# Attention heads of a decoder layer: product banks emptied in mid-step into two buffers, scores issued one and a half tiles ahead

## The reference, cut to what matters

```python
proj = h @ w_in                      # q, k, v of both groups, 16 heads of 64
# group A, 8 "stick-breaking" heads (called SB here)
z = q @ k.T * d ** -0.5              # strictly causal
weights = exp(log_sigmoid(z) + later)    # later: sum of log_sigmoid(-z) over later keys before q
o = weights @ v
# group B, 8 rotary heads with dilated windows (called DIL here)
q, k = rotary(q), rotary(k)
o = softmax mixture over three (window, dilation) patterns of q @ k.T, times v
```

## Time and profile before

| what | value |
|---|---|
| median of 3 runs | 2114.16 us (2113.18 to 2114.74) |
| the profiled execution's own time | 2112.07 us |
| its span, first to last instruction | 2110.3 us |
| PE busy over the span | 1929.9 us (91%) |
| DVE, ACT, POOL busy | 1250.9, 903.0, 731.9 us |
| mean granted clock of TensorE | 0.961 |
| stretch of the heads' steps | about 724 to 1330 us |

### The profile page before, as it was taken

The page is one execution under the profiler, slowest core; times in us unless marked ns, Lnnn a source line. Parts: engine busy times, 40 slices in busy tenths (PEclk is TensorE's granted clock), DMA queues, the critical chain, the costliest instruction groups (busy, mean ns, idle before and its releaser), DMA issues. The chain is left out here.

```text
span 2110.3 us, 25935 instructions
## 1 busy us (share of the span) xinstructions
PE 1929.9 (91%) x9224; PEld 1580.6 (75%) x9224; DVE 1250.9 (59%) x1665; ACT 903.0 (43%) x1451; POOL 731.9 (35%) x490
## 2 busy tenths in 40 slices
PE   5899999999998978978888876797899999999998
PEld 4788888888887767767667665586688888888886
DVE  6855555555556266657666578336955556555555
ACT  6433333333335345545545556305433333333334
POOL 2656556540000241231231235402656656540000
PEclk9999999999999989989989997898999999999999
DMA  3443534458664210111111012512443534458663
GB/s 141 161 163 134 195 130 172 158 204 294 194 195 159 70 42 26 36 40 29 30 40 40 25 36 70 185 40 80 144 165 132 195 147 156 174 190 309 194 195 140
DMA packets 95574, 275.93 MB, mean 131 GB/s; under 512 B 10480, under 2 KB 14704, under 8 KB 89840
## 3 DMA queue, kind: packets, MB, share of 16 engines
q1 hardware_dynamic: 95472, 274.59, 38.2%
HBM read 190.14 MB, written 80.22 MB: 128 GB/s over the span
## 5 line engine op out<-in xcount | busy, mean ns | idle before, releaser
L703 PE MATMUL banks<-ffn_x_operands_hi 128*128 128x512 f32 x616 | 239.8, 389 | 0.0
L706 PE MATMUL banks<-ffn_x_operands_hi,ffn_x_operands_lo 128*128 128x512 f32 x616 | 239.7, 389 | 0.0
L705 PE MATMUL banks<-ffn_x_operands_lo,ffn_x_operands_hi 128*128 128x512 f32 x616 | 239.6, 389 | 0.0
L1376 PE MATMUL banks<-first_hi,w_hi 128*128 128x512 f32 x384 | 163.6, 426 | 58.9 <-ACT heads_rot_in L1113 42.8
L1244 DVE TENSOR_TENSOR heads_wt<-banks,heads_wt 128x512 fp32r<-128x512 f32 (+1 forms) x160 | 101.0, 633 | 171.3 <-ACT heads_wt L1091 171.1
L991 POOL TENSOR_TENSOR w_lo<-w_raw,w_hi 128x1024 fp32r<-128x1024 f32 x22 | 52.5, 2385 | 362.3 <-ACT w_hi L1055 362.3
L984 POOL TENSOR_TENSOR scaled_rows<-scaled_rows,heads_stay 128x128 f32<-128x128 f32 (+7 forms) x64 | 86.0, 1350 | 237.5 <-DVE heads_stay L1204 237.5
L401 ACT ACTIVATE scaled_rows<-banks 128x512 f32<-128x512 f32 x132 | 78.9, 598 | 203.4 <-PE banks L690 203.4
L516 DVE TENSOR_TENSOR scaled_rows<-banks,scaled_rows 128x512 f32<-128x512 f32 x132 | 91.2, 691 | 117.7 <-PE banks L690 73.5
L1091 ACT ACTIVATE heads_wt<-banks 128x512 fp32r<-128x512 f32 (+1 forms) x160 | 88.8, 555 | 166.2 <-PE banks L1427 165.4
L1378 PE MATMUL banks<-first_hi,w_lo 128*128 128x512 f32 x384 | 157.9, 411 | 0.0
(11 more groups left out here) (183 smaller groups left out, 4854.6 us busy)
## 6 DMA issues: line engine op xcount, KB each, us to landing
w_raw<-in_ffn_w_gate SPq DMA_DIRECT2D x22, 1024.0 KB, 6.8
ffn_up_raw<-in_ffn_w_up SPq DMA_DIRECT2D x22, 1024.0 KB, 6.2
ffn_down_raw<-in_ffn_w_down SPq DMA_DIRECT2D x22, 1024.0 KB, 4.9
down_operands<-ffn_down_raw SPq DMA_DIRECT2D x22, 1024.0 KB, 7.3
w_raw<-h_operands SPq DMA_DIRECT2D x52, 256.0 KB, 2.9
ffn_up_raw<-h_operands SPq DMA_DIRECT2D x52, 256.0 KB, 3.0
ffn_down_raw<-h_operands SPq DMA_DIRECT2D x50, 256.0 KB, 3.0
w_raw<-in_w_in SPq DMA_DIRECT2D x24, 512.0 KB, 3.9
```

The source lines that it names most:

```text
L703: pe.matmul(out, hi[:, 0, tok], hi[:, 1, :], start=(opens and c == 0), stop=False, skip_group_check=True)
L705: pe.matmul(out, hi[:, 0, tok], lo[:, 1, :], start=False, stop=False, skip_group_check=True)
L706: last = pe.matmul(out, lo[:, 0, tok], hi[:, 1, :], start=False, stop=(c == NP - 1), skip_group_check=True)
L1376: pe.matmul(out, hi[:, k, :], norm.xn_hi[:, k, cols], start=(k == 0), stop=False)
```

## The change

Three things change together. First, `UNITS` is rewritten so that products 0 to 4 end before a step's bank (bank 0 in step 1, bank 1 in steps 2 to 5) and no longer behind its last one; `ENDS` keeps the same steps. Second, every q and k product is copied by ACT at once into `qk_raw[j % 2]` and the PSUM bank is free with that copy, for both kinds; the SB kind's high part is then made by ACT from this buffer, and its low part by POOL instead of DVE. `rot_swap` becomes two buffers as well. Third, PE issues `scores(s+2)` within step s, ahead of its last bank (behind the only bank in steps 0 and 1) and before that bank's projection units, where before `scores(s+1)` opened the step.

```diff
-UNITS = ((2, 2), (2, 2), (2, 4, 2), (3, 2, 3), (2, 1, 3, 2), (2, 1, 3, 2), (2, 1, 3, 1, 0), (0, 0, 1, 0, 0))
+UNITS = ((3, 2), (3, 2), (3, 3, 2), (3, 3, 2), (3, 3, 2, 0), (3, 3, 2, 0), (2, 2, 1, 0, 0), (0, 0, 1, 0, 0))
...
-        rot_in, rot_swap, rot_out = sb("rot_in", [P, HALF]), sb("rot_swap", [P, HALF]), sb("rot_out", [P, HALF])
+        qk_raw = [sb(f"qk_raw{i}", [P, HALF]) for i in range(2)]
+        rot_swap, rot_out = [sb(f"rot_swap{i}", [P, HALF]) for i in range(2)], sb("rot_out", [P, HALF])
...
+            def projected_lo(it, j):
+
+                piece, half = PRODUCTS[j]
+                cols = slice(half * HALF, (half + 1) * HALF)
+                pool.wait_ge(sb_hi_done, ROTATED * it + j + 1)
+                pool.tensor_tensor(qk_lo[SB_KIND][piece][:, cols], qk_raw[j % 2][:, :],
+                                   qk_hi[SB_KIND][piece][:, cols].bitcast(F32), ALU.subtract).then_inc(sb_split, 1)
...
-                if project and kind1 == DIL_KIND and ENDS.get(s, HALVES) < ROTATED:
-                    rotate_cos(it1, ENDS[s])
+                if project and ENDS.get(s, HALVES) < ROTATED:
+                    if kind1 == DIL_KIND:
+                        rotate_cos(it1, ENDS[s])
+                    else:
+                        projected_lo(it1, ENDS[s])
...
-                elif kind == SB_KIND:
-                    act.activation(qk_hi[kind][piece][:, cols], b.ps[:, bank, :], ACT.Copy
-                                   ).then_inc(sb_hi_done, 1)
                 else:
-                    act.wait_ge(rot_split, 1 + ROTATED * it + j)
-                    act.activation(rot_in[:, :], b.ps[:, bank, :], ACT.Copy).then_inc(proj_free, 1)
+                    if kind == DIL_KIND:
+                        act.wait_ge(rot_split, 1 + ROTATED * it + j - (j > 0))
+                    if kind == SB_KIND and (j > 1 or not (isinstance(it, int) and it == 0)):
+                        act.wait_ge(sb_split, ROTATED * it + j - (j > 0))
+                    act.activation(qk_raw[j % 2][:, :], b.ps[:, bank, :], ACT.Copy).then_inc(proj_free, 1)
+                if piece != V and kind == SB_KIND:
+                    act.wait_ge(proj_free, 1 + HALVES * run(it, kind) + j + 1)
+                    act.activation(qk_hi[kind][piece][:, cols], qk_raw[j % 2][:, :], ACT.Copy).then_inc(sb_hi_done, 1)
...
-            def projected_lo(it, j, bank=BANK_PROJ):
...
+            def scores_ahead(it, kind, s, last):
+
+                if s + 2 < STEPS:
+                    scores(it, kind, s + 2)
+                elif not last:
+                    scores(*pair_of(it, kind, 1), s + 2 - STEPS)
+
             def step(it, kind, s, proj=True, last=False):
                 it1, kind1 = pair_of(it, kind, 1)
-                nit, nkind, ns = (it, kind, s + 1) if s < STEPS - 1 else (it1, kind1, 0)
-                if not (last and s == STEPS - 1):
-                    scores(nit, nkind, ns)
+                early = max(banks_of(s) - 1, 1)
...
                 for j in range(banks_of(s)):
+                    if j == early:
+                        scores_ahead(it, kind, s, last)
                     if proj:
                         project(it1, kind1, *units_between(s, j))
                     turn_weights(it, kind, s, j, proj)
                     values_behind(it, kind, s, j, 2)
+                if early == banks_of(s):
+                    scores_ahead(it, kind, s, last)
                 if proj:
                     project(it1, kind1, *units_between(s, banks_of(s)))
...
             scores(0, SB_KIND, 0)
+            scores(0, SB_KIND, 1)
```

More of the change, by code:

```diff
@@ L850, in heads_block @@
         proj_ready, proj_free = sem("proj_ready"), sem("proj_free")
-        sb_hi_done = sem("sb_qk_hi_done")
-        rot_swapped, rot_cos, rot_sin, rot_sum = (sem(f"rot_{n}") for n in ("swapped", "cos", "sin", "sum"))
+        sb_hi_done, sb_split = sem("sb_qk_hi_done"), sem("sb_qk_split")
+        rot_swapped = [sem(f"rot_swapped{i}") for i in range(2)]
+        rot_cos, rot_sin, rot_sum = (sem(f"rot_{n}") for n in ("cos", "sin", "sum"))
         rot_hi_done, rot_split = sem("rot_hi_done"), sem("rot_split")
@@ L915, in swap_halves @@
                         dst = head * HEAD + (1 - part) * 32
-                        sp.dma_start(rot_swap[dst:dst + 32, :], rot_in[src:src + 32, :]
-                                     ).then_inc(rot_swapped, 16)
+                        sp.dma_start(rot_swap[j % 2][dst:dst + 32, :], qk_raw[j % 2][src:src + 32, :]
+                                     ).then_inc(rot_swapped[j % 2], 16)
             def store_part(it, kind, part):
@@ L999, in rotate_cos @@
                 pool.wait_ge(rot_split, 1 + n)
-                pool.tensor_tensor(rot_out[:, :], rot_in[:, :], cos_sb[:, half * HALF:(half + 1) * HALF],
+                pool.tensor_tensor(rot_out[:, :], qk_raw[j % 2][:, :], cos_sb[:, half * HALF:(half + 1) * HALF],
                                    ALU.mult).then_inc(rot_cos, 1)
+            def projected_lo(it, j):
[4 more added lines that the diff above has]
+                                   qk_hi[SB_KIND][piece][:, cols].bitcast(F32), ALU.subtract).then_inc(sb_split, 1)
             def step(it, kind, s, project=True, last=False):
@@ L1033, in one_run @@
                         split_out_weights(s)
-            split_weights(0, 0, V)
-            split_weights(0, 1, Q)
+            for j in range(HALVES):
+                if j < ROTATED:
+                    projected_lo(0, j)
+                if j == 2:
+                    split_weights(0, 0, V)
+                if j == 3:
+                    split_weights(0, 1, Q)
             pool.wait_ge(tables_ready, 1)
@@ L1267, in values_out @@
                                   ).then_inc(o_copied, 1)
-            def projected_lo(it, j, bank=BANK_PROJ):
[L1271 to L1274, removed]
-                                  qk_hi[SB_KIND][piece][:, cols].bitcast(F32), ALU.subtract
-                                  ).then_inc(proj_free, 1)
             def rotate(it, j):
@@ L1281, in rotate @@
                 n = ROTATED * it + j
[L1282 to L1283 removed]
+                dve.wait_ge(rot_swapped[j % 2], 64 * (ROTATED // 2 * it + j // 2 + 1))
+                dve.tensor_tensor(rot_swap[j % 2][:, :], rot_swap[j % 2][:, :], sin_sb[:, cols], ALU.mult).then_inc(rot_sin, 1)
                 dve.wait_ge(rot_sin, n + 1)
                 dve.wait_ge(rot_cos, n + 1)
[L1286 removed]
+                dve.tensor_tensor(rot_out[:, :], rot_out[:, :], rot_swap[j % 2][:, :], ALU.add).then_inc(rot_sum, 1)
             def rotated_lo(it, j):
@@ L1309, in step @@
                 for j in range(banks_of(s)):
-                    if project and kind1 == SB_KIND and ends_before(s, j) and ENDS[s] < ROTATED:
-                        projected_lo(it1, ENDS[s])
                     weights_lo(it, kind, s, j, project)
@@ L1325, in step @@
                     rotated_lo(*rot)
-                if project and kind1 == SB_KIND and ends_before(s, banks_of(s)) and ENDS[s] < ROTATED:
-                    projected_lo(it1, ENDS[s])
                 if last and s == STEPS - 1:
@@ L1386, in scores @@
                     if kind == SB_KIND:
-                        pe.wait_ge(proj_free, 1 + HALVES * run(it, kind) + (2 if s == 0 else 4))
+                        pe.wait_ge(sb_split, ROTATED * it + (2 if s == 0 else 4))
                     else:
```

5 lines of the change are left out of this document (removed).

## The result

| what | before | after |
|---|---|---|
| median | 2114.45 us (2113.18 to 2114.74, 4 runs) | 2179.72 us (2178.85 to 2180.09, 4 runs) |
| ratio | | 1.0309, 95% interval 1.0291 to 1.0327 |
| profiled execution, its span | 2112.07, 2110.3 us | 2179.71, 2177.9 us |
| TensorE's mean granted clock | 0.961 | 0.951 |

What follows compares the result with a forecast made beforehand. PE was taken to bound DIL runs, a ring of in-order engines SB runs. 2112.07 + 18.6 (DIL) + 8 (SB) = 2138.7 us profiled, 2141 us as median; the 8-in-10 range was 2090 to 2165 us.

Steps and rivals of the forecast that it cites:

- The added wait: DIL steps 0 to 3: PE stands at early scores until the next tile's second head is read, 7.9 us per run.
- What was taken away: PE's waits for `rot_in`, v and low-part copies end: 12.8 us per SB run; with a score wait, 3.4 per DIL run.
- DIL runs: New waits 7.9 us against 3.4 gone, plus 1.7 for the clock: +6.2 us per run, +18.6 for three.
- SB runs: Three parts of the run, 2.7 - 1.8 - 0.6, plus 1.7 for the clock: +2.0 us per run, +8 for four.
- the last run: Without units, transposes about 2 us later in steps 2, 3, about 1.5 earlier in 4 to 6: 0, bounds -5 and +5.
- the transitions: No own term; from the fourth rotation to an SB run's end, the v copy no longer precedes the gates: -0.6 us.
- Rival D: DVE and POOL collide over POOL's new low parts, 6.4 us in each of three DIL runs: 2160 us, chance 0.05.
- The clock: One 3.4 us spell at 1.2 GHz per DIL run, behind the 3.0 us wait, costs 1.7 us; SB runs also +1.7.
- The ring: In-order engines waiting on each other bound SB runs from tile 2's transposes to the fourth rotation: 51.7 against 53.5 us.
- B: `rotated_hi` is ready when ACT comes, gates are not late; SB runs lose 15.7 us each: about 2070 us, chance 0.22.
- C: No change: no clock spells (-15 us) and a ring 3 us shorter per run: 2114 us, chance 0.09.
- The signs to look for: Expected profile: raw-copy waits under 1 us, score waits on gates and maximum, DIL clock spells, run lengths, ACT idle 4 us.

Runs made afterwards that it cites:

- fourth experiment: The changed kernel with the SB kind's low parts made by DVE again instead of POOL: 2177.58 us, ratio 1.0298.
- the first experiment: The changed kernel with scores(s+1) opening step s again; new `UNITS`, early copies, two buffers and POOL's low part stay: 2082.19 us, ratio 0.9848.

## Why the prediction was right in sign and wrong in size

**The added wait, right.** "It waits until both heads of tile s+1 are read. But the second head is read only behind the copy of bank (s, 0), which PE has just transposed." That holds, in place and in size: forecast 0.8, 3.0, 2.5, 1.6 us in a DIL run, measured 0.83, 3.02, 2.69, 1.68. Reading the heads in another order takes the DIL loss away, and confining the early scores to steps 4 to 6 nearly all of it in SB and DIL runs and half of it in the last.

**What was taken away, right in after.** No unit waits for a copy any more. Alone, this part brings 32 us, but not as forecast: it leaves 11.0 us of waits for copies, takes 7 to 10 us from an SB run and makes a DIL run 1.0 us longer, not 3.4 shorter. In after those 11.0 us are gone too; that PE stands at the scores while the copies are made is my reading and was not tested.

**Which terms failed.** The sum for the profiled execution is 41.0 us too low (2138.7 for 2179.71). DIL runs have 18.5 of that (18.6 forecast, 37.1 measured), SB runs 10.0 (8 and 18.0), the last run 8.6 (0 and 8.6), the transitions 3.6, for which there was no term. The steps that failed are the two short waits called covered, the spells counted as one, DVE's outputs left out in SB runs, and the gain expected in the last run.

**DIL runs, term too small: +6.2 forecast, +12.3 measured.** Waits and clock explain it. PE's idle time in the run rose from 3.4 us before to 11.7 (71.02 - 59.36). Of this, 8.2 us were the four foreseen waits, and 2.1 were in steps 4 and 5, of which I wrote "have three units and a whole bank between and are covered". They are covered while a normalisation takes 0.6 us, not 2.7. Another 1.4 us of idle time stayed, where I had counted all 3.4 as gone. *Rival D named the mechanism, at 6.4 us per run, and looked at the wrong operation.* I asked what POOL would newly do, and that makes no difference (fourth experiment). What collides is what POOL did already, moved in time by `UNITS`. The remaining 4.1 us are busy time (59.36 - 55.26), of which the clock has 3.4.

**The clock, one spell for two.** The forecast put one spell of 3.4 us behind the wait of 3.0 us. There is one behind each of the two longest waits, 3.02 and 2.69 us. Busy time by stretch, after, the 3.4 us behind the starts at 1000.56 and 1010.07:

```profile
1000.80:1004.20 3.40, 3.40 (x11) 2.26 (x10) 1.85 (x6) 0.64 (x2) 0.00 (x0) 0.50 0.85 199
1010.80:1014.20 3.40, 3.40 (x15) 2.62 (x12) 0.00 (x0) 0.00 (x0) 0.00 (x0) 0.53 0.00 0
```

In both PE is busy all through, at 1.2 of 2.4 GHz, and loses half of it: 3.4 us per run against the 1.7 taken. The two spells lay inside the bounds that I gave ("two or three spells, 5 us"), and the forecast took one.

**SB runs, term too small: +2.0 forecast, +4.2 in the run shown, 18.0 for four against 8.** The ring was the right picture, and the waits at the scores came out *shorter* than forecast, 12.5 us for 15.3. Missing were two other waits. Waits of PE, after, the SB run from 896.76 to 979.38 us:

```profile
PE banks L1411 <- ACT heads_stay L1083: 12.5, 6, 3.9
PE banks L1454 <- DVE heads_o_stage L1287: 2.9, 1, 2.9
PE banks L1433 <- DVE heads_wt L1265: 1.9, 2, 1.3
```

The same stretch before has 10.7 us for `rot_in`, 2.0 for v and 0.7 for POOL, 13.4 in all, against 17.3 here: +3.9 us. The 4.8 us behind DVE are not the scores' doing: with the scores in their old place they are there too (4.0 and 0.8 us). With the old `UNITS` and the same buffers there are 1.1 us of them, so they come with the new `UNITS`. I had counted only the chain through ACT and gave DVE's outputs no new wait. The clock's term of +1.7 did not come: PE's busy time is 64.3 us before and 64.5 after in this run, at 0.89 and 0.90.

**Transitions.** I counted each run up to its last step, and "from there to the run's end" at -0.6. The stretch from step 7's mark to the next run's step 0 grew instead by 0.9 us four times. Busy time by stretch, after:

```profile
979.38:988.02 8.64, 7.58 (x43) 6.85 (x44) 4.50 (x13) 5.58 (x12) 1.44 (x1) 0.75 0.00 0
```

Before it is 7.75 us with PE busy for 5.72 at clock 1.00. What is new is a spell at 1.2 GHz from 976.87 to 983.70, behind the wait of 2.90 us for DVE's output that ended at 975.93. Two experiments place it: with the scores in their old place the stretch still takes 8.59 us at clock 0.68, and with the old `UNITS` as well 7.76 us at 1.00. It comes with the new `UNITS`.

**The last run, term with its bounds too small: 0 with -5 to +5 forecast, +8.6 measured.** The forecast set two scores of about 2 us later against three banks of about 1.5 us earlier. Waits of PE, after, the last run:

```profile
PE banks L1433 <- DVE scaled_rows L1251: 11.6, 9, 2.5
PE banks L1411 <- DVE heads_row_max L1236: 8.7, 6, 2.5
PE banks L1454 <- DVE heads_o_stage L1287: 2.7, 2, 1.6
```

Before it is 4.7, 3.7 and 8.6 us. PE is late at the transposes as well as at the scores; I take it that without units nothing uses the lateness up, which no experiment isolates. The gain in steps 4 to 6 is there only in the 8.6 that fell to 2.7, and on the whole it is a loss: early scores from step 4 on alone make this run 5.1 us longer (61.15 for 56.04). The clock fell from 0.74 to 0.70.

**Rivals.** B, "the ring opens", got 0.22. For after it is wrong, and yet it describes the first experiment: SB runs of 69 us at clock 0.92 to 0.97. "SB runs near 70 us with the clock near 1.0" is what the buffers and the new `UNITS` do when the scores stay. I priced the two parts together, in the ring: -1.8 us from the start of tile 2's transposes to the fourth rotation. In fact the one part takes 9 us off an SB run (78.38 to 69.07) and the other puts 13.5 on. C has no support, and its clock spells come to 12 us by the sum's own terms (seven of 1.7), not 15.

**The signs to look for.** Right: no wait on the raw copy; 51.8 us at the scores for gates (40 to 60 forecast); clock spells in DIL runs; ACT idle before each `rotated_hi`, though for 2.0 to 4.8 us and not always 4. Wrong: 39.5 us for the maximum (20 to 30 forecast), DIL runs of 79.4 us from step 0's mark to the next run's (71 to 75), and SB runs of 89.9 to 91.3 us in the same way (84 to 90).

**What stays open.** How the 13.5 us that the scores' place costs an SB run divide between waits and clock is known only in parts. Taking `rotated_hi` out of the way removes 24 us of gate waits over all runs, but 22 return through POOL, and that return was not taken away by itself. Why `UNITS` moves the weight split in DIL runs was not followed link by link either; the runs show only that it does.

## What to carry to other kernels

Issuing work earlier into a double buffer can move a wait instead of removing it: look up where in its own queue the engine that frees the buffer reads it, and compare that with the work that still lies behind the issue on the first engine. Split a change into its parts before it is judged, since here -32 and +97 us were in one diff. When a change shifts the timing of a step, ask not only what each engine newly does beside the others, but which old operations now fall beside one another.

## What the runs showed of the hardware

- DVE and POOL held each other up by whole instructions, in both directions. A normalisation on SBUF of 0.55 us takes 2.73 us when POOL's split of 2.39 us starts just ahead of it; POOL's split of 2.38 us takes 5.05 when a scan and a rotation of DVE fall inside it, although by the recorded starts it began first.
- The short POOL operations of 1.29 us, beside DVE operations that read PSUM, made no measurable difference to having DVE do them (1.0309 against 1.0298).
- Pauses of PE of 3.02 and 2.69 us were each followed by some 3.4 us at 1.2 GHz in a DIL run at 2.4 GHz otherwise; those of 1.68 us and less in the same run were not. The length of the pause alone doesn't settle it: in the SB run such a spell (915.43 to 918.84) followed a pause of 1.96 us.
